# Two squared-relu MLPs: the relu moved to ScalarE without the norm's factor, the factor squared applied as a column of numbers where results are added

## The chip, the cores and the metric

The kernel runs on one core of a Trainium2 chip. The metric is the device time of one execution in microseconds (us). A core has TensorE (PE in the profile; PEld is its weight load), VectorE (DVE), ScalarE (ACT), GpSimd (POOL) and a queue processor for transfers (SP, SyncE). Sums of matmuls are collected in PSUM, eight banks of 512 float32 numbers in each of 128 partitions.

## The reference

The whole program is two transformer blocks. The change touches only the MLPs of the second block, of which there are two. All values are float32, with 512 tokens of width 1024 and a hidden width of 4096:

```
def _rmsnorm(x, g):
    y = xf * lax.rsqrt(jnp.mean(xf * xf, axis=-1, keepdims=True) + EPS)
    return (y * g).astype(x.dtype)

def _sqrelu_mlp(h, w1, w2):
    u = jax.nn.relu(h @ w1)
    return (u * u) @ w2

for i in range(DEPTH_2):                     # 2: retention, then chunk attention
    ...
    h = h + _sqrelu_mlp(_rmsnorm(h, mlp_norm_g[i]), mlp_w1[i], mlp_w2[i])
```

Below, r is the factor rsqrt(mean(x²) + eps). It is one number per token and positive, so relu(r·a) = r·relu(a), and r² can be pulled out of the square and out of the second product, which sums over the hidden width and not over tokens.

## The kernel before

**Precision.** Every float32 product is made of three TensorE products of a high and a low part: high·high, low·high, high·low (L925 to L927, helper `three`). So each weight and each activation is first split: ScalarE copies it to a rounded type (`w_hi`, `hid_hi`, `hn_hi`), and VectorE or GpSimd subtracts that from the original (`w_lo`, `hid_lo`, `hn_lo`).

**An MLP** (`mlp` on each engine; stage A runs from about 1048 to 1379 us, stage B from about 1619 to 1949 us) goes through 4 groups of 1024 hidden columns. In a group there are first four "ups" (m = 0 to 3, `mlp_up`): each makes 256 hidden columns for all tokens in a pair of PSUM banks, Y (banks 0, 1) for even m and X (banks 2, 3) for odd m, with 48 matmuls. The activations are x times the gain, without r. Then come seven second products of 24 matmuls each in the order A11, A12, S3, M, A21, S1, S4 (`PRODUCTS`): a Strassen-like scheme with seven instead of eight products, whose sums of blocks of the squared activations are T3, T2, T4, T1 (VectorE, `t3` to `t1`) and whose sums of weight blocks are made by accumulating transfers that POOL issues (`weight_sums`, L892, L896, L898) and by VectorE (`m_sum`, L3063).

**After an up**, VectorE takes the pair of banks, makes max(·, 0) times r (`relu`, L3022, one instruction of 128x1024 into `sq`), and tells with `mlp_up_taken`; ScalarE squares that into `u_squared` (L2169), which lies in the place of `x`; ScalarE then makes the high part (L2178) and VectorE the low part (L3029). r is there as a row for all tokens (`r_bc`), since tokens lie along the columns here.

**The second product** has tokens along the partitions. Its results are added to `x_tok` (x transposed, in `o_buf`) by VectorE's `take` (L3072). In each group there are nine: Q1, Q7, Q6, Q2, Q4 with two banks at once (128x1024), and Q5, Q5+1, Q3, Q3+1 with one bank (128x512). PE waits for some of them before it opens a bank again: M for Q1, A21 for Q7, S1 for Q6, and S4, whose two token tiles share X with S1, for Q5 and Q5+1 (L1445).

**How r is made.** ScalarE squares x, VectorE adds up the eight tiles in `ssq`, and splits the sum in two rounded halves (L2369, L2371). PE spreads their sum to all partitions with two matmuls with ones (`stat_halves`, L968), one before k = 3 and one before k = 4 of the second up of group 0 (`in_second`); ScalarE makes exp(-0.5·ln(·)) of the 128x512 result (`rsqrt`, L1671, L1674). VectorE waits for r before anything else in the MLP (L3074).

**The transposes** of x to `x_tok` also lie in group 0: PE does f = 0 to 3 in the second up, ahead of k = 4 to 7, and f = 4 to 7 in the third up, ahead of k = 0 to 3 (`to_tokens`, L1467, four 128x128 transposes each, banks 4 to 6), and ScalarE copies each to `x_tok` (`token_copy`, L2160). In ScalarE's order copies 0 to 3 stand ahead of the first square and copies 4 to 7 behind its high part. Up m waits at its start until up m-2 is taken (L1407), since it uses the same banks.

**Orders** on each engine are written out by hand; every wait is on a semaphore. The squared r as a column of numbers is already known elsewhere: the retention head uses `stat_columns` (L973): four matmuls with a 128x128 tile of `ssq` as weights and one column of ones, so that token t of each tile lands in partition t.

## Time and profile before

| | us |
|---|---|
| median of 3 timed runs (1957.20 to 1957.37) | 1957.34 |
| the profiled execution, its own time | 1958.46 |
| the profiled execution, its span | 1956.7 |
| PE busy in the span | 1938.3 (99%) |
| DVE busy | 1205.2 (62%) |
| ACT busy | 880.1 (45%) |
| POOL busy | 603.0 (31%) |

A row of a timeline has the start in us from the span's start, the duration in us, engine, line, operation, output and inputs, shape and count; brackets at its end give the idle time of the engine before it and what ended that. Matmuls overlap: a 128x512 matmul is shown with 0.39 us, but the next one starts 0.227 us after it. So PE's pace is read from the distances between starts, not from durations. The same holds for VectorE and ScalarE, where the next instruction starts about 0.08 to 0.11 us before the end of the one before it.

### The profile page before, as it was taken

The page shows a single profiled execution, that of the slowest core. Times are in us where ns is not written, and L with a number is a line of the kernel's source. Part 1 is how long each engine was busy: PE and PEld are TensorE (multiplying, and loading weights), DVE is VectorE, ACT ScalarE, POOL GpSimd, SP SyncE. Part 2 cuts the span into 40 slices and gives each one's busy share as a digit, 9 for nine tenths or more (in the row PEclk, how much of TensorE's full clock was granted, in tenths as well). Part 3 has the DMA queues.
Part 4 walks back from the last instruction along what each step waited for, and adds up shares of the span by engine and source line. Part 5 has one row for each costly group of instructions (what it writes and reads, how often), then busy time and mean ns, then how long its engine had stood idle before and what let it go on. Part 6 is the DMA issues. An engine that isn't in the chain of part 4 may idle for free.

```text
span 1956.7 us, 23662 instructions
## 1 busy us (share of the span) xinstructions
PE 1938.3 (99%) x9216; PEld 1609.5 (82%) x9216; DVE 1205.2 (62%) x1701; ACT 880.1 (45%) x1284; POOL 603.0 (31%) x442
## 2 busy tenths in 40 slices
PE   8999999999999999999999999999999999999998
PEld 7877878888888888888888888888888888888886
DVE  7667763332257854545455857668566676866757
ACT  7445543332234552525245534444455555444435
POOL 2333645455455335353533000000333341000000
PEclk9999999999999999999999999999999999999999
DMA  5312367276322322222225557465322226746553
GB/s 164 94 44 76 97 98 116 93 123 112 94 86 87 119 76 94 79 87 85 86 86 151 128 173 179 123 172 129 107 86 85 86 65 183 173 128 172 122 179 86
DMA packets 166338, 221.31 MB, mean 113 GB/s; under 512 B 4640, under 2 KB 120096, under 8 KB 166112
## 3 DMA queue, kind: packets, MB, share of 16 engines
q1 hardware_dynamic: 151728, 190.52, 30.0%
q0 software_dynamic: 12928, 25.71, 7.7%
q10 hardware_dynamic: 1584, 3.74, 4.3%
q8 instruction: 66, 1.08, 0.2%
q14 instruction: 32, 0.26, 0.0%
HBM read 214.84 MB, written 4.72 MB: 112 GB/s over the span
## 4 chain that ended last, share of the span: by engine, by line
PE 89%; DVE 4%; ACT 2%; issue 2%; POOL 1%; DMA 1%; SPq 0%; DVEq 0%; ACTq 0%; POOLq 0%
PE ps L925 28%; PE ps L927 28%; PE ps L926 28%; PE ps L1097 1%; PE ps L1127 1%; POOL w_lo L819 1%; PE ps L1136 1%; PE ps L1137 1%; PE ps L1114 1%; DVE scr L2601 1%; DMA aux<-in_mlp_w 0%; PE ps L1467 0%; ACT w_hi L1612 0%; ACT w_hi L1630 0%; DVE w_lo L3011 0%
## 5 line engine op out<-in xcount | busy, mean ns | idle before, releaser
L819 POOL TENSOR_TENSOR w_lo<-raw,w_hi 128x512 fp32r<-128x512 f32 x376 | 529.8, 1440 | 667.4 <-ACT w_hi L1612 667.4
L925 PE MATMUL ps<-hn_hi,w_hi 128*128 128x512 f32 x1524 | 602.4, 395 | 2.2 <-DVE hn_lo L2710 1.7
L927 PE MATMUL ps<-hn_hi,w_lo 128*128 128x512 f32 x1524 | 593.8, 390 | 0.0
L926 PE MATMUL ps<-hn_lo,w_hi 128*128 128x512 f32 x1524 | 593.7, 390 | 0.0
L925 PEld LDWEIGHTS ps<-hn_hi,w_hi 128*128 128x128 f32 x1524 | 286.4, 188 | 66.3 <-issue 4.1
L927 PEld LDWEIGHTS ps<-hn_hi,w_lo 128*128 128x128 f32 x1524 | 286.2, 188 | 60.6
L926 PEld LDWEIGHTS ps<-hn_lo,w_hi 128*128 128x128 f32 x1524 | 286.5, 188 | 58.9 <-issue 1.7
L1612 ACT ACTIVATE w_hi<-raw 128x2048 fp32r<-128x2048 f32 (+1 forms) x98 | 186.0, 1898 | 286.9 <-PE ps L927 286.8
L1630 ACT ACTIVATE w_hi<-raw 128x1024 fp32r<-128x1024 f32 x112 | 116.1, 1056 | 205.2 <-PE ps L927 205.0
L925 PE MATMUL ps<-w_hi,hid_hi 128*128 128x512 f32 x456 | 177.7, 390 | 0.2
L926 PE MATMUL ps<-w_lo,hid_hi 128*128 128x512 f32 x456 | 177.4, 389 | 0.0
L927 PE MATMUL ps<-w_hi,hid_lo 128*128 128x512 f32 x456 | 177.4, 389 | 0.0
L3011 DVE TENSOR_TENSOR w_lo<-raw,w_hi 128x1024 fp32r<-128x1024 f32 x104 | 126.2, 1223 | 67.6 <-ACT w_hi L1630 59.3
L926 PE MATMUL ps<-hid_lo,w_hi 128*128 128x512 f32 x392 | 152.7, 390 | 0.0
L925 PE MATMUL ps<-hid_hi,w_hi 128*128 128x512 f32 x376 | 147.8, 393 | 0.1
L927 PE MATMUL ps<-hid_hi,w_lo 128*128 128x512 f32 x376 | 146.4, 389 | 0.0
L2414 DVE TENSOR_TENSOR scr<-ps,scr 128x512 f32<-128x512 f32 x42 | 27.1, 686 | 138.7 <-PE ps L927 135.3
L896 POOL DMA_DIRECT2D raw<-in_mlp_w x8 | 10.3, 1286 | 305.5 <-DMA raw<-in_mlp_w 305.5
L925 PEld LDWEIGHTS ps<-w_hi,hid_hi 128*128 128x128 f32 x456 | 85.6, 188 | 18.6 <-DVE hid_lo L2537 0.6
L927 PEld LDWEIGHTS ps<-w_hi,hid_lo 128*128 128x128 f32 x456 | 85.6, 188 | 17.8
L926 PEld LDWEIGHTS ps<-w_lo,hid_hi 128*128 128x128 f32 x456 | 85.6, 188 | 17.8
L3029 DVE TENSOR_TENSOR hid_lo<-x,hid_hi 128x512 fp32r<-128x512 f32 (+1 forms) x96 | 74.7, 778 | 32.6 <-ACT hid_hi L2178 31.8
(357 smaller groups left out, 2849.8 us busy)
## 6 DMA issues: line engine op xcount, KB each, us to landing
raw<-in_mlp_w SPq DMA_DIRECT2D x56, 1024.0 KB, 5.4
raw<-in_ret_w_in SPq DMA_DIRECT2D x24, 1024.0 KB, 5.2
aux<-in_mlp_w POOLq DMA_DIRECT2D x16, 1024.0 KB, 8.9
raw<-in_att_w_in SPq DMA_DIRECT2D x12, 1024.0 KB, 5.5
raw<-in_w_gate SPq DMA_DIRECT2D x11, 1024.0 KB, 5.4
raw<-in_w_up SPq DMA_DIRECT2D x11, 1024.0 KB, 5.3
raw<-in_w_down SPq DMA_DIRECT2D x8, 1024.0 KB, 8.0
raw<-in_ret_w_out SPq DMA_DIRECT2D x8, 1024.0 KB, 5.0
```

The lines of the kernel that those rows point to most:

```text
L819: ins = pool.tensor_tensor(w_lo[:, slot, at], raw[:, slot, at], w_hi[:, slot, at].bitcast(F32), ALU.subtract)
L925: pe.matmul(o, hi, rhs_hi, start=start, stop=False, skip_group_check=True)
L926: pe.matmul(o, hi, rhs_lo, start=False, stop=False, skip_group_check=True)
L927: return pe.matmul(o, lo, rhs_hi, start=False, stop=stop, skip_group_check=True)
L1097: ins = pe.matmul(a.score_ps(b, t), q[:, t * P:(t + 1) * P], k[:, 0:(t + 1) * P], start=(n == 0), stop=(n == last), skip_group_check=True)
L1114: ins = pe.matmul(a.score_ps(b, t), q[:, t * P:(t + 1) * P], k[:, 0:(t + 1) * P], start=(nth == 0 and n == 0 and t != 0), stop=(nth == 1 a ...
L1127: ins = pe.transpose(a.trans_ps(b, j)[:, (t - j) * P:(t - j + 1) * P], a.score_sb(b, t)[:, j * P:(j + 1) * P], ident[:, :])
L1612: act.activation(w_hi[:, c.slot, 0:columns], raw[:, c.slot, 0:columns], ACT.Copy)\
L1630: act.activation(w_hi[:, ml.slot(g, b), HALVES[half]], half_source(ml, g, b, half), ACT.Copy)\
L2414: dve.tensor_tensor(dst, ps[:, g.bank(m), :], r, ALU.mult).then_inc(pair_free[g.pair], 1)
L3011: dve.tensor_tensor(w_lo[:, slot, at], half_source(ml, g, b, half), w_hi[:, slot, at].bitcast(F32), ALU.subtract).then_inc(s["w_lo_ready"], 1)
L3029: dve.tensor_tensor(lo_part, src, hi_part.bitcast(F32), ALU.subtract).then_inc(s["mlp_lo"], 1)
```

## The change

The MLP's statistics are now made by `stat_columns` (before k = 3 of the second up, into bank 7), so neither rounded halves nor a spread row are made. ScalarE makes r² from it in three small instructions (ln, exp with scale -1, and a negated copy) into `r_two`: four columns of r², four of -r². The relu of each up is done by ScalarE, from the PSUM banks straight into `u_squared`, and its square in place. VectorE's `relu` and its wait for r go. `take` becomes one `scalar_tensor_tensor` for each bank: bank times the token tile's column of ±r², plus `x_tok`. VectorE waits once per MLP for `r_two`, ahead of the first half of M in group 0.

```diff
-    def __init__(self, prev, n, split, halves=False, by_tokens=False):
+    def __init__(self, prev, n, split, halves=False, by_tokens=False, columns=False):
-        self.index = prev.index + (not by_tokens) if prev else 0
+        self.index = prev.index + (not by_tokens and not columns) if prev else 0
-N_MLPA = Norm(N_RET, 8, 8, halves=True)
+N_MLPA = Norm(N_RET, 8, 8, columns=True)
-N_MLPB = Norm(N_ATT, 8, 8, halves=True)
+N_MLPB = Norm(N_ATT, 8, 8, columns=True)
+        r_two = sb("r_two", [P, 8])
-            def stat_columns(norm):
+            def stat_columns(norm, bank=6):
-                    if 3 <= k < 5:
-                        stat_halves(norm, k - 3)
+                    if k == 3:
+                        stat_columns(norm, 7)
+                def r_for_tokens():
+                    act.wait_ge(s["col_stat"], 2 + ml.layer)
+                    act.activation(r_two[:, 0:4], ps[:, 7, 0:4], ACT.Ln, scale=1.0 / D, bias=eps[:, 0:1])\
+                        .then_inc(s["col_ln"], 1)
+                    act.wait_ge(s["col_ln"], 2 * ml.layer + 2)
+                    act.activation(r_two[:, 0:4], r_two[:, 0:4], ACT.Exp, scale=-1.0).then_inc(s["mlp_r"], 1)
+                    act.wait_ge(s["mlp_r"], 2 * ml.layer + 1)
+                    act.activation(r_two[:, 4:8], r_two[:, 0:4], ACT.Copy, scale=-1.0).then_inc(s["mlp_r"], 1)
                 def squared(g, m):
-                    act.wait_ge(s["mlp_up_taken"], ml.ups(g, m))
+                    bank, u = (Y, X)[m % 2], u_squared[:, 2 * m:2 * m + 2, :]
+                    act.wait_ge(s["group_done"], ml.done(g, m, 1))
                     if g == 0:
                         act.wait_ge(s["x_t"], turned + 2 * m + 2)
-                    act.activation(u_squared[:, 2 * m:2 * m + 2, :], sq, ACT.Square).then_inc(s["mlp_sq"], 1)
+                    act.activation(u, ps[:, bank:bank + 2, :], ACT.Relu).then_inc(s["mlp_up_taken"], 1)
+                    act.wait_ge(s["mlp_up_taken"], ml.ups(g, m))
+                    act.activation(u, u, ACT.Square).then_inc(s["mlp_sq"], 1)
                         if g == 0 and m == 0:
-                            rsqrt(norm, D)
+                            r_for_tokens()
                             for f in range(4):
                                 token_copy(f)
                         squared(g, m)
-                def relu(g, m):
-                    ...
-                    dve.scalar_tensor_tensor(sq, ps[:, bank:bank + 2, :], 0.0, r_bc.unsqueeze(1).to_broadcast([P, 2, S]),
-                                             ALU.max, ALU.mult).then_inc(s["mlp_up_taken"], 1)
                 def take(g, product, b, half, f, t, bank, op, tiles=slice(0, 2)):
                     ...
-                    o = token_block(f, t)[:, tiles, :]
-                    dve.tensor_tensor(o, o, ps[:, bank + tiles.start:bank + tiles.stop, :], op).then_inc(s["mlp_taken"], 1)
-                dve.wait_ge(s["norm_r"], norm.index + 1)
+                    for n in range(tiles.start, tiles.stop):
+                        o, at = token_block(f, t)[:, n, :], 2 * t + n + (0 if op is ALU.add else 4)
+                        ins = dve.scalar_tensor_tensor(o, ps[:, bank + n, :], r_two[:, at:at + 1], o, ALU.mult, ALU.add)
+                    ins.then_inc(s["mlp_taken"], 1)
                         half_lo(ml, g, m + 2, 0)
-                        relu(g, m)
                         half_lo(ml, g, m + 2, 1)
                     if g == 0:
                         dve.wait_ge(s["x_copied"], kept + KD)
+                        dve.wait_ge(s["mlp_r"], 2 * ml.layer + 2)
```

The numbers that `col_ln` waits for elsewhere are renumbered; nothing else moves.

## Rows read from the trace of the kernel before

**Rows 1.** The page, part 1: busy time of PE, share, instructions.
```profile
PE 1938.3 (99%) x9216; PEld 1609.5 (82%) x9216; DVE 1205.2 (62%) x1701; ACT 880.1 (45%) x1284; POOL 603.0 (31%) x442
```

**Rows 2.** Windows, all but the ends of MLP A: start:end, length, busy us (instructions), granted clock, DMA share.
```profile
1061.00:1378.00 317.00, 317.00 (x1424) 262.76 (x1423) 217.81 (x230) 144.90 (x171) 14.12 (x11) 1.00 0.57 150
```

**Rows 3.** Timeline, PE: the first statistics matmul in the second up, and the next.
```profile
1061.45 0.39 PE L968 MATMUL ps<-sq_halves,ones_r 128*128 128x512 f32 x1
1061.68 0.39 PE L925 MATMUL ps<-hn_hi,w_hi 128*128 128x512 f32 x1
```

**Rows 4.** Timeline, PE: the column statistics of the retention head.
```profile
662.17 1.03 PE L977 MATMUL ps<-ones_r,scr 128*128 128x1 f32 x8
663.06 0.48 PE L968 MATMUL ps<-sq_halves,ones_r 128*128 128x512 f32 x1
663.38 0.39 PE L925 MATMUL ps<-hn_hi,w_hi 128*128 128x512 f32 x1
```

**Rows 5.** Timeline, PE and PEld: transposes 3 and 4, and the third up's start.
```profile
1068.75 0.60 PE L1467 MATMUL ps<-ident,x 128*128 128x128 f32 x4
...
1070.58 0.60 PE L1467 MATMUL ps<-ident,x 128*128 128x128 f32 x4
...
1070.35 0.59 PEld L1467 LDWEIGHTS ps<-ident,x 128*128 128x128 f32 x4
```

**Rows 6.** Timeline, ACT, in the same stretch; then DVE's first relu.
```profile
1069.39 0.60 ACT L2160 ACTIVATE o_buf<-ps 128x512 f32<-128x512 f32 x1 [1.23 <-PE ps L1467]
1069.88 1.05 ACT L2169 ACTIVATE x<-scr 128x1024 f32<-128x1024 f32 x1
...
1066.44 1.22 DVE L3022 SCALAR_TENSOR_TENSOR scr<-ps,scr 128x1024 f32<-128x1024 f32 x1
```

**Rows 7.** Timeline, DVE, attention's start: instructions with a column of numbers, from PSUM.
```profile
1378.13 1.41 DVE L3143 SCALAR_TENSOR_TENSOR hn_lo<-ps,gains,hn_hi 128x512 fp32r<-128x512 f32 x2 [1.29 <-ACT hn_hi L2227]
1379.46 0.68 DVE L3072 TENSOR_TENSOR o_buf<-o_buf,ps 128x512 f32<-128x512 f32 x1
```

**Rows 8.** Timeline, DVE, MLP A, group 1: the takes, and the weight halves of S4.
```profile
1188.45 1.22 DVE L3072 TENSOR_TENSOR o_buf<-o_buf,ps 128x1024 f32<-128x1024 f32 x1
1189.58 1.22 DVE L3063 TENSOR_TENSOR aux<-aux,hid_rest 128x1024 f32<-128x1024 f32 x1
...
1201.69 1.22 DVE L3072 TENSOR_TENSOR o_buf<-o_buf,ps 128x1024 f32<-128x1024 f32 x1
1203.28 2.36 DVE L3011 TENSOR_TENSOR w_lo<-aux,w_hi 128x1024 fp32r<-128x1024 f32 x2 [0.37 <-ACT w_hi L1630]
1205.55 2.01 DVE L3072 TENSOR_TENSOR o_buf<-o_buf,ps 128x1024 f32<-128x1024 f32 x2
```

**Rows 9.** Timeline, POOL, ACT and PEld, same group: transfer for S4, S4's first weights.
```profile
1193.46 1.28 POOL L898 DMA_DIRECT2D aux<-in_mlp_w  x1 [19.48 <-DVE w_lo L3011]
...
1202.18 2.17 ACT L1630 ACTIVATE w_hi<-aux 128x1024 fp32r<-128x1024 f32 x2 [3.27 <-DMA aux<-in_mlp_w]
...
1208.24 0.19 PEld L925 LDWEIGHTS ps<-w_hi,hid_hi 128*128 128x128 f32 x1
```

**Rows 10.** Timeline, DVE and PEld, MLP B, group 1: the same place.
```profile
1777.64 2.01 DVE L3072 TENSOR_TENSOR o_buf<-o_buf,ps 128x1024 f32<-128x1024 f32 x2
...
1779.94 0.19 PEld L925 LDWEIGHTS ps<-w_hi,hid_hi 128*128 128x128 f32 x1
```

**Rows 11.** Timeline, PE, PEld, DVE, MLP B, group 0: the same place.
```profile
1697.96 0.39 PE L927 MATMUL ps<-w_hi,hid_lo 128*128 128x512 f32 x1
1698.44 0.50 PE L925 MATMUL ps<-w_hi,hid_hi 128*128 128x512 f32 x1
...
1696.38 2.80 DVE L3072 TENSOR_TENSOR o_buf<-o_buf,ps 128x1024 f32<-128x1024 f32 x3
...
1698.43 0.19 PEld L925 LDWEIGHTS ps<-w_hi,hid_hi 128*128 128x128 f32 x1 [0.51 <-DVE o_buf L3072]
```

**Rows 12.** Timeline, ACT and DVE, the last 12 us.
```profile
1944.60 0.29 ACT L2329 ACTIVATE small<-small 128x1 f32<-128x1 f32 x1 [0.36 <-DVE small L3317]
```

More of the change, by code:

```diff
@@ L298 @@
  gain_pair old_hi old_lo apart_done apart_scaled apart_sum gate_old_done gate_e_hi gate_e_lo gate_sig gate_read
- mlp_up_taken mlp_sq mlp_sum mlp_hi mlp_lo mlp_taken s3_in s3_added a21_in s1_added m_summed s4_added
+ mlp_up_taken mlp_r mlp_sq mlp_sum mlp_hi mlp_lo mlp_taken s3_in s3_added a21_in s1_added m_summed s4_added
  att_in_hi att_in_lo tab_scaled ffn_silu ffn_part token_sq token_sum r_diagonal r_spread r_row fin_weighed fin_left fin_right fin_whole""".split()
@@ L971, in stat_halves @@
                     ins.then_inc(s["norm_stat"], 1)
-            def stat_columns(norm):
+            def stat_columns(norm, bank=6):
                 pe.wait_ge(s["norm_acc"], norm.acc0 + norm.n - 1)
                 for t in range(4):
-                    ins = pe.matmul(ps[:, 6, t:t + 1], ssq[:, t * P:(t + 1) * P], ones[:, 0:1], start=True, stop=True)
+                    ins = pe.matmul(ps[:, bank, t:t + 1], ssq[:, t * P:(t + 1) * P], ones[:, 0:1], start=True, stop=True)
                 ins.then_inc(s["col_stat"], 1)
@@ L1656, in rsqrt_columns @@
                     .then_inc(s["col_ln"], 1)
-                act.wait_ge(s["col_ln"], nth + 1)
+                act.wait_ge(s["col_ln"], 2 * nth + 1)
                 act.activation(r_col[:, 0:4], r_col[:, 0:4], ACT.Exp, scale=-0.5).then_inc(s["col_r"], 1)
@@ L2330, in token_rsqrt @@
                     .then_inc(s["col_ln"], 1)
-                act.wait_ge(s["col_ln"], 3 + t)
+                act.wait_ge(s["col_ln"], 5 + t)
                 act.activation(r_col[:, t:t + 1], r_col[:, t:t + 1], ACT.Exp, scale=-0.5).then_inc(s["col_r"], 1)
@@ L3014, in mlp @@
             def mlp(ml, norm, kept, finish):
-                def relu(g, m):
-                    bank = (Y, X)[m % 2]
-                    dve.wait_ge(s["group_done"], ml.done(g, m, 1))
-                    if ml.ups(g, m) > 1:
-                        dve.wait_ge(s["mlp_sq"], ml.ups(g, m) - 1)
-                    dve.scalar_tensor_tensor(sq, ps[:, bank:bank + 2, :], 0.0, r_bc.unsqueeze(1).to_broadcast([P, 2, S]),
-                                             ALU.max, ALU.mult).then_inc(s["mlp_up_taken"], 1)
                 def part_lo(g, what, n):
```

## The prediction, made before the changed kernel was run

> **What bounds the kernel now.** I read the busy times first. TensorE is busy for 99% of the span [rows 1], so the end is set by its own work, and no other engine's load counts unless it makes PE wait. Then the windows: over nearly the whole of MLP A, PE is busy for all of 317.00 us, at a granted clock of 1.00 (the upper of the two levels, 2.4 GHz), while VectorE is at 218 us and ScalarE at 145 us [rows 2]. Then PE's timeline. Its 128x512 matmuls start 0.227 us apart [rows 3], and in both MLPs I found only one place where this pace is lost to a wait: in MLP B, group 0, at S4, where the next matmul starts 0.476 us after the last one instead of 0.227, and its weight load waited 0.51 us for a `take` [rows 11]. So there is at most 0.4 us of stall that the change could take away, and the question is what it adds to PE's stream and which new waits reach PE.
>
> **The PE's own work.** Removed per MLP: two 128x512 matmuls with ones, 2 x 0.227 = 0.45 us [rows 3]. Added: four column matmuls of the kind that the retention head has. They are eight instructions there, from 662.17 to 663.06, 0.89 us, and the matmul after them is followed at 0.32 us instead of 0.227 [rows 4], another 0.09. Net +0.53 us per MLP, +1.06 us for two. All of it is on the path, since PE is. The bounds: 0.89 us may hold a short wait for the sum of squares, so +0.3 to +0.6 each. The sum is there early enough in both MLPs, so nothing is waited for.
> What the row shows is 0.11 us for each one-column matmul. The Trainium skill (TensorE: Matmul & The Clock Gate, section Back-to-back issue gap) gives about 60 cycles for 1 to 64 columns, which is 25 ns at 2.4 GHz; with that the four would cost an estimated 0.2 us and the change would save about 0.15 us of PE per MLP. The same page (section LDWEIGHTS) has about columns/1.2 ns for a weight load, 107 ns for 128, and that is what the trace agrees with: every column matmul brings its own 128x128 weights.
>
> **The third up waits for ScalarE.** This is the new wait. Up 2 of group 0 may start only when up 0 has been taken. Before, VectorE did that at 1066.44 to 1067.66 [rows 6], three us early. Now it is the relu of ScalarE, and in ScalarE's order it stands behind `token_copy` 0 to 3, the last of which waits for the fourth set of transposes. In the trace: those transposes start at 1068.75, the third up's first instruction (transposes 4) at 1070.58, its weight load at 1070.35 [rows 5]. ScalarE starts copy 3 at 1069.39, that is 0.64 after the transposes, and can start the next instruction at 1069.88 [rows 6]. That next one is now the relu. No row shows a relu of 128x1024 from PSUM; the square of that size takes 1.05 from SBUF, the copy of 128x512 from PSUM 0.60 [rows 6]. I take 1.03, with 1.0 and 1.22 (VectorE's [rows 6]) as the ends. It ends at 1070.91. A weight load follows its release by 0.05 us (1698.38, the end of the second of the three takes there, to 1698.43 [rows 11]), so it starts at 1070.96 instead of 1070.35. Of such a delay 0.1 to 0.2 is swallowed, because the weight load runs ahead of its matmul: in [rows 11] a weight load 0.47 late cost PE 0.25 at the first matmul and 0.11 at the second. So 0.61 late costs about 0.5 us. All times shift together when the column matmuls come ahead, so the distance stays. +0.5 us per MLP, **+1.0 us** for two; bounds 0.3 and 0.7 each. Up 3's wait for up 1 has about 3 us to spare, as has A12's wait for up 3: 0 us. Queued behind the relu on ScalarE are the square, the high part and copies 4 to 7; transposes 7 wait for copy 4 (done at about 1073.7, needed at 1076.4): 0 us.
>
> **ScalarE in the other ups.** From group 1 on VectorE took a finished up at once, and ScalarE meanwhile made the high half of a weight block. Now the relu is behind that half: square and parts come about 0.9 us later. The parts of up 3 are needed only at A12's second half, 3.5 us after they are ready, and in the products ScalarE then waits for PE again (S3's second half), which takes up the delay. 0 us. The ceiling, were that cover gone, is 0.9 us for each group.
> A rule that speaks against the change: the Trainium skill (ScalarE: Activation LUTs, section Rules for kernel authors) says to put relu on VectorE. It argues with bfloat16 modes; here the rows show float32 work of the same size at 1.22 us on VectorE and 1.05 us on ScalarE [rows 6], so the rule costs nothing in this kernel; the order on ScalarE does.
>
> **VectorE's takes.** VectorE loses 4 relus of 1.22 us per group, but they lie among the ups, where nothing waits for it. The cost is in the products. Two instructions with a column of numbers from PSUM occupy 1.33 us (1378.13 to 1379.46 [rows 7]) and the second ends 1.41 after the first starts; the 128x1024 `take` occupies 1.13 to 1.14 and takes 1.22 [rows 8]. So +0.2 us for each of the five two-bank takes and 0.06 for a one-bank take (0.745 against 0.69). From Q1 to Q2 VectorE has next to no idle time, so four takes (Q1, Q7, Q6, Q2) move its arrival at S4's weight halves by 0.78 us; the 0.37 to 0.46 us of idle time there [rows 8] swallow part of it. The transfer that makes S4's weights starts behind VectorE's low half of M [rows 9], which only Q1 delays: +0.2. Then Q4 and Q5 lie between these halves and PE's S4: +0.25 more at Q5's end.
> Group 1 of MLP A: Q2 starts at 1201.69; 1.135 + 0.78 later, at 1203.61, VectorE comes to S4 instead of at 1203.28: +0.33, and Q5 ends 0.58 later. It ended at 1207.56; S4's weight load started at 1208.24 [rows 8, 9] and needs 0.05, so the slack was 0.63: 0 us. Worked out so for the eight groups (first and most critical: [rows 8 to 10]) the slack is 0.62 to 0.66 in five, with shifts of 0.58 to 0.65; 0.38 in group 0 of MLP A, with a shift of 0.49, where the 0.115 that is swallowed just covers it; 0.24 in group 1 of MLP B (Q5 ends at 1779.65, load at 1779.94 [rows 10]), where the transfer leads and the shift is 0.45: 0.45 - 0.24 - 0.115 = 0.1 us; and none in group 0 of MLP B, which stalls already: +0.45 us. **Sum +0.55 us**, bounds 0 (a landing that is early again) and 3 (all groups 0.4 late).
>
> **The tail.** In the last group Q4 ends 0.55 later (0.35 at S4's halves and 0.2 in itself); ScalarE's squares for the final norm follow it, and had 0.36 us to spare before VectorE's mean [rows 12]: +0.2 at the end. The last two takes are one-bank takes in VectorE's chain: +0.12. Together +0.3 us, bounds 0.1 and 0.6.
>
> **At nothing:** VectorE's cast and subtraction for the halves, and its wait for r, go from where PE never waited. Three small instructions for r² (0.7 us) replace two of 128x512 on ScalarE, in time that it spends waiting for transposes. VectorE's wait for r² comes 40 us after it is made.
>
> **Sum:** 1.06 + 1.0 + 0.55 + 0.3 = 2.9 us. The profiled execution would go from 1958.46 (span 1956.7) to 1961.4 (span 1959.6). Its time is 1.1 us above the median of the timed runs; I add to the median: 1957.34 + 2.9 = 1960.2, or +0.15%. A measurement of this kernel tells about 0.2% (3.9 us) from no change, so this is "the same".
>
> **The rivals.**
> *A slower kernel (above 1961.3).* The takes reach PE in every group. This decides from the point where Q5 ends 0.75 us later (slack 0.64 plus the 0.115 swallowed), and my shifts are only 0.1 to 0.2 below that in five groups. If a two-instruction take occupied 1.5 instead of 1.33 us, S4's halves would come at +1.5 - 0.4, Q5 at +1.45, and each group would pay about 0.5 to 0.7 us: 8 x 0.5 = 4 us and with the other terms 1957.3 + 2.4 + 4 = 1963.7. For it: margins this small. Against it: POOL, which shares VectorE's work in other stages, is busy for 14 of 317 us here [rows 2].
> *Cheaper than said (1957.5 to 1959.3).* The new wait costs 0.3 and the column sums 0.3 per MLP, and S4 is not reached: 0.6 + 0.6 + 0 + 0.2 = 1.6, 1958.9. It needs a quicker relu and an earlier landing of the one late transfer.
> *Faster (below 1953.4).* It would have to take 4 us off PE's own stream. The freed 39 us of VectorE (32 x 1.22) can give back only the 0.4 us stall [rows 2, 11]: 1957.0 even if nothing were added.
> *It does not do what it says:* r² could be late and hold VectorE at its wait; it is made by about 1064 and needed at about 1105.
>
> **How the numbers follow.** Forecast (1959.3 to 1961.2) 0.63, cheaper 0.15, slower 0.19, faster 0.03. The range leaves out no more than 2 in 10: 1958.3 (all lower bounds: 0.6 + 0.6 + 0 + 0.1 gives 1.3, and a little is left out) to 1963.2. Same: 0.63 + 0.15 = 0.78.
>
> **What would show it.** Right: after the change L977 has 24 instructions in all and L968 two fewer per MLP; PE waits twice for ScalarE's relu, ahead of transposes 4, some 0.5 us each; takes in pairs of 0.745 us at 0.665 apart; S4 waits in MLP B for `take` in groups 0 and 1. VectorE's busy time falls by about 28 us and ScalarE's rises by about 31. Wrong: a PE wait at A12 or for part lows (ScalarE's order), waits at S4 in all eight groups (slower rival), or a relu far from 1.03 us.

## The result, and the profile after

| | before | after |
|---|---|---|
| median, 20 runs each | 1957.45 | 1960.31 |
| lowest to highest | 1956.83 to 1958.90 | 1959.02 to 1962.73 |
| profiled execution, own time | 1958.46 | 1959.21 |
| its span | 1956.7 | 1957.4 |

The ratio is 1.0015, with a 95% interval of 1.0008 to 1.0022: 2.9 us more, where the sum had said 2.9. Two things in the table are not explained by that sum. The spans of the two profiled executions differ by 0.7 us only, and the times of the changed kernel lie almost twice as far apart as those of the one before. All medians and ratios here and below leave out two executions that took far longer than all others, one of "relu early" (3955 us) and one of the kernel before beside it (6937 us).

The page of the changed kernel, part 1; it answers to [rows 1]:
```profile
PE 1938.8 (99%) x9228; PEld 1610.0 (82%) x9228; DVE 1174.0 (60%) x1705; ACT 909.2 (46%) x1318; POOL 604.3 (31%) x442
```
PE has 12 instructions more: in each MLP eight column instructions for two of 128x512. VectorE lost 31.2 us, ScalarE gained 29.1.

The timeline of the changed kernel, PE, at the statistics of MLP A (start, duration, engine, line, operation, tiles, shape, count). It answers to [rows 3, 4]:
```profile
1060.93 0.39 PE L928 MATMUL ps<-hn_hi,w_lo 128*128 128x512 f32 x1
1061.16 0.94 PE L978 MATMUL ps<-ones_r,scr 128*128 128x1 f32 x8
1061.97 0.49 PE L926 MATMUL ps<-hn_hi,w_hi 128*128 128x512 f32 x1
1062.29 0.40 PE L927 MATMUL ps<-hn_lo,w_hi 128*128 128x512 f32 x1
```
The eight take 0.81 us from their first start to the next matmul, and that one is followed 0.32 instead of 0.227 later. I laid all matmuls of this trace beside those of before, one by one, and followed the difference of their starts. Over the statistics it grows by 0.46 us in MLP A and 0.47 in MLP B.

The same stretch some 9 us later, ACT, PE and PEld (in brackets the idle time before, and what ended it). It answers to [rows 5, 6]:
```profile
1069.57 0.60 ACT L2161 ACTIVATE o_buf<-ps 128x512 f32<-128x512 f32 x1 [1.24 <-PE ps L1468]
1070.07 1.02 ACT L2181 ACTIVATE x<-ps 128x1024 f32<-128x1024 f32 x1
...
1070.53 0.40 PE L928 MATMUL ps<-hn_hi,w_lo 128*128 128x512 f32 x1
1071.14 0.66 PE L1468 MATMUL ps<-ident,x 128*128 128x128 f32 x4 [0.21 <-ACT x L2181]
...
1071.14 0.42 PEld L1468 LDWEIGHTS ps<-ident,x 128*128 128x128 f32 x4 [0.64 <-ACT x L2181]
```
This is the new wait. The third up's first instruction starts 0.61 after the matmul ahead of it. The difference of the starts grows by 0.43 us here, and by 0.43 in MLP B: 0.37 of it at the first of the four transposes, 0.06 at the second.

The timeline of the changed kernel in MLP B, group 2, from the transfer that makes S4's weights to PE's S4. It answers to [rows 8, 9, 11]:
```profile
1846.90 1.28 POOL L899 DMA_DIRECT2D aux<-in_mlp_w  x1 [19.26 <-DVE w_lo L3025]
...
1856.44 2.01 ACT L1631 ACTIVATE w_hi<-aux 128x1024 fp32r<-128x1024 f32 x2 [4.27 <-DMA aux<-in_mlp_w]
...
1855.51 1.40 DVE L3078 SCALAR_TENSOR_TENSOR o_buf<-ps,r_two,o_buf 128x512 f32<-128x512 f32 x2
1857.53 2.36 DVE L3025 TENSOR_TENSOR w_lo<-aux,w_hi 128x1024 fp32r<-128x1024 f32 x2 [0.62 <-ACT w_hi L1631]
1859.81 3.12 DVE L3078 SCALAR_TENSOR_TENSOR o_buf<-ps,r_two,o_buf 128x512 f32<-128x512 f32 x4
...
1862.12 0.50 PE L926 MATMUL ps<-w_hi,hid_hi 128*128 128x512 f32 x1 [0.23 <-DVE o_buf L3078]
1862.46 0.40 PE L927 MATMUL ps<-w_lo,hid_hi 128*128 128x512 f32 x1
```
The transfer is issued at 1846.90, and ScalarE starts on its result 9.54 us later; VectorE's halves, then Q4 and Q5, follow without a gap, and PE waits. It loses 0.56 us here and 0.17 in group 1. Group 0, the one place with a loss before (0.38 us, [rows 11]), loses nothing.

Waits of the weight load from 1060 us to the end, changed kernel (what is waited for, us in total, times, longest), the rows that are new:
```profile
PEld ps L1468 <- ACT x L2181: 1.3, 2, 0.6
PEld ps L926 <- DVE o_buf L3078: 1.0, 2, 0.7
```
So the terms of the profiled execution are 0.93 (columns) + 0.86 (relu) + 0.35 (S4: 0.73 less 0.38) + 0.19 (from the start of the last matmul to the end: 8.28 against 8.09) = 2.3 us. Its span grew by 0.7, because three waits of some 0.4 us in the attention, which the kernel before had in its profile, aren't in this one (1.3 us), and the start was 0.3 us shorter. The start varies by more than that between executions; how far the attention's waits are chance is taken up in the last section.

### The profile page after: what moved, and what is told of

Same layout as the page of the kernel before. It is cut to its first block, busy times and chain, and to the rows that moved or that the text cites. A ratio compares the mean times of both kernels' runs of the same rounds, so it can differ in the third digit from the quotient of the medians.

```text
span 1957.4 us, 23691 instructions
## 1 busy us (share of the span) xinstructions
PE 1938.8 (99%) x9228; PEld 1610.0 (82%) x9228; DVE 1174.0 (60%) x1705; ACT 909.2 (46%) x1318; POOL 604.3 (31%) x442
## 4 chain that ended last, share of the span: by engine, by line
PE 90%; DVE 4%; ACT 3%; issue 2%; POOL 1%; DMA 1%; SPq 0%; DVEq 0%; POOLq 0%; ACTq 0%
PE ps L926 28%; PE ps L928 28%; PE ps L927 28%; PE ps L1098 1%; PE ps L1128 1%; POOL w_lo L820 1%; PE ps L1137 1%; PE ps L1138 1%; PE ps L1115 1%; DMA aux<-in_mlp_w 0%; ACT scr L1842 0%; ACT w_hi L1613 0%; PE ps L1468 0%; DMA raw<-in_w_in 0%; DVE hn_lo L2877 0%
```

## The experiments

Each kernel ran 11 times (the columns twice 9 times). "Before" is the median of the kernel before on the same chip; the spans are those of the profiled executions. A difference of the spans alone is not much to go by: the first 12 us alone were up to 2.3 us longer in some executions than in others.

| kernel | median | before | ratio, 95% | span |
|---|---|---|---|---|
| the change again | 1960.81 | 1958.26 | 1.0013 [1.0004, 1.0022] | 1958.8 |
| relu early | 1960.65 | 1958.53 | 1.0011 [1.0001, 1.0020] | 1956.8 |
| takes alone | 1959.50 | 1958.53 | 1.0005 [0.9996, 1.0015] | 1957.7 |
| plain takes | 1959.74 | 1958.53 | 1.0006 [0.9997, 1.0015] | 1957.9 |
| columns twice | 1963.42 | 1958.53 | 1.0024 [1.0014, 1.0034] | 1961.1 |
| relu early, Q4 later | 1958.95 | 1958.26 | 1.0003 [0.9994, 1.0012] | 1957.6 |
| before, Q4 later | 1958.30 | 1958.26 | 1.0000 [0.9991, 1.0009] | 1956.1 |
| statistics over tokens, Q4 later | 1957.77 | 1958.26 | 0.9998 [0.9989, 1.0007] | 1955.2 |
| the same again | 1957.52 | 1958.02 | 0.9997 [0.9988, 1.0006] | 1955.4 |
| statistics over tokens, Q4 first | 1959.63 | 1958.02 | 1.0008 [0.9999, 1.0017] | 1959.0 |

**The relu early.** The theory is that the new wait is one of order on ScalarE: the first relu stands behind the copies. The relu now goes between copies 1 and 2, and nothing else moves:
```diff
                             for f in range(4):
+                                if f == 2:
+                                    taken_relu(g, m)
                                 token_copy(f)
```


> The changed kernel with one order changed: ScalarE does the relu of up 0 of group 0 between token copies 1 and 2 instead of after copy 3. Theory A (the loss is a sum of three separate PE-side terms: column sums 0.5 us per MLP, the wait of the third up for the relu 0.4 us per MLP, the takes at S4 and in the tail 0.6 to 0.9 in all): both PE waits ahead of transposes 4 (weight load idle 0.6 us each in the changed kernel) are gone, PE is 0.4 us earlier from there in each MLP, and the median falls by 0.75 us, from 1960.3 to 1959.5. Theory B (nearly all of the 2.9 us comes from the takes, and a wait that is removed ahead of them is only paid later, at S4): the waits are gone, the median stays at 1960.3 within 0.2. Theory C (the loss is ScalarE's later squares): no change either, 1960.3.

ACT and PE of this kernel at the same place:
```profile
1066.63 1.02 ACT L2181 ACTIVATE x<-ps 128x1024 f32<-128x1024 f32 x1
1067.96 0.60 ACT L2161 ACTIVATE o_buf<-ps 128x512 f32<-128x512 f32 x1 [0.31 <-PE ps L1468]
1069.79 0.60 ACT L2161 ACTIVATE o_buf<-ps 128x512 f32<-128x512 f32 x1 [1.23 <-PE ps L1468]
...
1070.75 0.39 PE L928 MATMUL ps<-hn_hi,w_lo 128*128 128x512 f32 x1
1070.98 0.60 PE L1468 MATMUL ps<-ident,x 128*128 128x128 f32 x4
```
The relu lies in a hole of ScalarE, 3.4 us earlier, the copies behind it still have to wait for PE, and transposes 4 start 0.23 after the matmul ahead of them. The wait is gone in both MLPs. So its cause is shown: the place in ScalarE's order, not the length of the relu. Nor is it paid back later: over the whole of MLP A the difference of the starts grows by 0.48 us here and by 0.89 in the change. The medians (+2.1 us here, +2.9 and +2.6 for the change) lean the same way but can't tell 0.86 us; the trace does.

**The takes alone.** The kernel before, with its takes made as in the change, and columns of +1 and -1 in place of r²:
```diff
-                    o = token_block(f, t)[:, tiles, :]
-                    dve.tensor_tensor(o, o, ps[:, bank + tiles.start:bank + tiles.stop, :], op).then_inc(s["mlp_taken"], 1)
+                    for n in range(tiles.start, tiles.stop):
+                        o, at = token_block(f, t)[:, n, :], 2 * t + n + (0 if op is ALU.add else 4)
+                        ins = dve.scalar_tensor_tensor(o, ps[:, bank + n, :], r_two[:, at:at + 1], o, ALU.mult, ALU.add)
+                    ins.then_inc(s["mlp_taken"], 1)
```


> The kernel before, with one part of the change: each take is done by one instruction per bank with a column of numbers, which holds 1 or -1, so the result is the same. Relu by VectorE with r, statistics by halves. Theory A: PE's stream is that of before up to S4; at S4 PE waits in the groups where the transfer leads (0.1 to 0.5 us each in one to three of eight groups), the tail is 0.2 to 0.3 longer: median 1957.45 + 0.9 = 1958.3. Theory B (the takes are nearly all of it): 1960. If takes cost PE nothing: 1957.5.

**The plain takes.** The opposite: the changed kernel with the takes of before. It leaves out the factor r², so what it adds to x is not the MLP's result; only its time is of use.
```diff
-                    for n in range(tiles.start, tiles.stop):
-                        o, at = token_block(f, t)[:, n, :], 2 * t + n + (0 if op is ALU.add else 4)
-                        ins = dve.scalar_tensor_tensor(o, ps[:, bank + n, :], r_two[:, at:at + 1], o, ALU.mult, ALU.add)
-                    ins.then_inc(s["mlp_taken"], 1)
+                    o = token_block(f, t)[:, tiles, :]
+                    dve.tensor_tensor(o, o, ps[:, bank + tiles.start:bank + tiles.stop, :], op).then_inc(s["mlp_taken"], 1)
```


> The changed kernel with the takes of before (one instruction for both banks, no factor), so r squared is left out of what is added to x; all else, the making of r squared too, is as in the changed kernel. Theory A: the column sums and the two waits for the relu stay, S4 waits only where it did before, the tail is that of before: 1960.3 - 0.9 = 1959.4, and the spread of the runs (1959.0 to 1962.7) shrinks towards that of before (1956.8 to 1958.9), since it is S4 that passes on when a transfer lands. Theory B: 1957.5. Theory C: 1960.3.

The takes by shape (duration in ns: shortest, median, longest; first and last start), the takes alone and then, in the kernel with the plain ones:
```profile
L3074 DVE SCALAR_TENSOR_TENSOR o_buf<-ps,r_two,o_buf x112: 673/748/755, 1107.6 to 1951.4; 128x512 f32<-128x512 f32 x112
```
```profile
L3077 DVE TENSOR_TENSOR o_buf<-o_buf,ps x72: 620/1214/1222, 1107.8 to 1951.7; 128x1024 f32<-128x1024 f32 x40, 128x512 f32<-128x512 f32 x32
```
The medians say +1.0 for the takes alone and +1.2 for all the rest of the change, each with an interval of some 2 us to either side; together that is 2.2, where the whole change has 2.6 and 2.9. What a take costs PE can't be read from them. It can from a table over the seven traces with this order of takes. The first number is the time from POOL's issue of S4's transfer to ScalarE's first high half, the second the loss of PE at S4 in that group. In MLP A the transfer always took 8.2 to 8.9 us and PE lost at most 0.03 in these kernels; these are the four groups of MLP B:
```
                              group 0       group 1       group 2       group 3
old takes   before            9.64  0.38    9.12  0       8.68  0       8.64  0
            plain takes       8.70  0       9.35  0       9.82  0.37    8.44  0
new takes   change            8.64  0       9.19  0.17    9.53  0.56    8.46  0
            change again      8.42  0       9.33  0.31   10.00  0.99    8.50  0
            relu early        8.78  0       8.83  0       9.70  0.72    8.34  0
            takes alone       8.60  0.02    9.51  0.51    8.44  0       8.61  0
            columns twice     8.30  0       8.77  0       9.30  0.31    9.66  0.69
```
With the new takes every transfer over 9.0 us costs about what it is over: 9.19 costs 0.17, 9.33 costs 0.31, 9.51 costs 0.51 and 10.00 costs 0.99. With the old takes one of 9.35 costs nothing and one of 9.82 costs 0.37; in group 0, the tightest, 9.64 costs 0.38. So what the new takes do is to lower what PE tolerates, outside group 0, from some 9.4 to 9.0 us, by about the 0.45 us that the prediction had as the shift where the transfer leads. Whether this also spreads the times is not shown: the plain takes were expected to lie closer together than the change, and their 11 runs lie over 2.6 us, those of the change again over 2.4, and those of the kernel before in the same session as the plain takes over 3.9.

Which group gets a late transfer has a pattern that the traces show. The DMA view of such a transfer in the kernel before (9.64 us) has, besides the transfer's own queue, this line (packets, MB, share):
```profile
q8 instruction: 1, 0.02, 0.6%
```
It is one packet of 16 KB that brings instructions. In the twelve traces there are 96 transfers for S4. In 23 of them such a packet falls between 4.9 and 8.0 us after the issue, and 22 of these are the ones that took 9.1 to 10.0 us, one took 8.8. All the other 73 took 8.2 to 8.8. None of the 48 in MLP A has a packet at that place, and none of them was late. Where the packets fall goes with the program: the change had both its late transfers in groups 1 and 2 in both of its profiles, and the first two kernels with statistics over tokens below, which are one kernel, both theirs in groups 0 and 1. No run moved a packet by itself, so that it makes the transfer late is argued from this agreement; and how late it is (9.53 and 10.00 for the same group of the same kernel) still varies between executions.

**The change again.** The same kernel, profiled a second time.

> The changed kernel once more, on the chip and beside the runs of the kernels of this call, for a second profile. Two things are asked. First, S4: theory A says that the group that makes PE wait there is chosen by when the transfer of its weights lands, so in another profile another group waits (landing after about 9.1 us), with the takes themselves unchanged. Second, attention: in the first profile PE waits less there for VectorE (L2615, one of the four multiplications behind GpSimd's start) than in the profile of before, 1.3 us in three places. If the change caused that, the second profile shows the same; if it is a race between the two engines that falls either way, it may show one to three of these waits again. Median as before: 1960.3, or the other kernels' shift on this chip added.

The timeline, VectorE, MLP B, group 2:
```profile
1858.97 2.36 DVE L3025 TENSOR_TENSOR w_lo<-aux,w_hi 128x1024 fp32r<-128x1024 f32 x2 [1.09 <-ACT w_hi L1631]
1861.25 3.12 DVE L3078 SCALAR_TENSOR_TENSOR o_buf<-ps,r_two,o_buf 128x512 f32<-128x512 f32 x4
```
VectorE sits idle for 1.09 us until the transfer is there (0.62 in the first profile), and PE loses 0.99. Columns 0.47 and 0.47, relu 0.43 and 0.43: these two repeat to 0.01 us. S4 doesn't: 1.30 in all against 0.73. But the expectation that another group would wait was wrong: they are groups 1 and 2 again. The span of this execution is 2.1 us above that of the first profile of before.

**The columns twice.** The four column matmuls once more, into columns of bank 7 that nobody reads:
```diff
                     if k == 3:
+                        for t in range(4):
+                            pe.wait_ge(s["norm_acc"], norm.acc0 + norm.n - 1)
+                            pe.matmul(ps[:, 7, 4 + t:5 + t], ssq[:, t * P:(t + 1) * P], ones[:, 0:1], start=True, stop=True)
                         stat_columns(norm, 7)
```


> The changed kernel with the four column matmuls done twice in each MLP (the first time into other columns of the same bank, which nobody reads). This measures their price by itself. Theory A: 0.11 us for each of eight instructions, because each loads its own 128x128 weights: PE falls back by 0.89 us more in each MLP, median 1960.3 + 1.8 = 1962.1. If a one-column matmul costs only its few columns (about 0.03 us each, 0.2 for the eight): 1960.3 + 0.4 = 1960.7.

PE of this kernel, at the statistics:
```profile
1062.06 0.39 PE L928 MATMUL ps<-hn_hi,w_lo 128*128 128x512 f32 x1
1062.29 0.95 PE L1480 MATMUL ps<-ones_r,scr 128*128 128x1 f32 x8
1063.10 1.03 PE L978 MATMUL ps<-ones_r,scr 128*128 128x1 f32 x8
1063.99 0.49 PE L926 MATMUL ps<-hn_hi,w_hi 128*128 128x512 f32 x1
```
Sixteen instructions in 1.70 us, 0.106 each. Beside the change the difference of the starts is 0.89 us larger in MLP A and 0.89 in MLP B. Against its own before the median stands at +4.9 us, the change's at +2.9 and +2.6: 2.0 to 2.3 more, of which the columns are 1.8. So four columns cost 0.89 us of PE, all of it on the path, and the step of the prediction that priced them from the retention head is shown right by a measurement of its own.

**Q4 later.** If PE loses at S4 because Q4 stands between the weight halves and Q5, then with Q5 and Q5+1 first, in groups 0 to 2, the loss goes, since PE's S4 needs these and not Q4. Made on the kernel with the early relu, and, as a control, on the kernel before (the counts that others wait for are renumbered in `taken`):
```diff
-                    take(g, ml.Q4, ml.A21, 1, 1, 0, Y, ALU.add)
+                    if last:
+                        take(g, ml.Q4, ml.A21, 1, 1, 0, Y, ALU.add)
...
                     take(g, ml.Q5 + 1, ml.S1, 1, 1, 1, X, ALU.subtract, slice(1, 2))
                     if not last:
+                        take(g, ml.Q4, ml.A21, 1, 1, 0, Y, ALU.add)
```


> The kernel of e1 (relu of up 0 between token copies 1 and 2), and in groups 0 to 2 of each MLP the two-bank take Q4 stands after Q5 and Q5+1 instead of ahead of them, so PE's S4 no longer waits for Q4. Theory A (the rest of the loss at S4 is the chain landing, weight halves, Q4, Q5): Q5 ends 1.4 to 1.5 us earlier in these groups, PE waits at S4 in none of the first three groups of an MLP even where the transfer lands after 9.5 us, and the median is 0.5 us below that of e1: 1.0 to 1.5 us above the kernel before. Rival (a take that is moved back makes PE wait at the next group's first up): waits there instead, no gain over e1.

> The kernel before with only that order changed: Q4 after Q5 and Q5+1 in groups 0 to 2. Theory A: its one wait at S4 (0.4 us in MLP B) goes, nothing else changes: 0.3 to 0.4 us faster than before, hardly more than noise in the median, but to be seen in the profile as no wait at S4 with a landing of up to 9.6 us. Rival: the wait returns at the next up.

VectorE, MLP B, group 2, in the kernel with the early relu and this order:
```profile
1858.73 2.36 DVE L3035 TENSOR_TENSOR w_lo<-aux,w_hi 128x1024 fp32r<-128x1024 f32 x2 [1.01 <-ACT w_hi L1633]
1861.01 0.75 DVE L3088 SCALAR_TENSOR_TENSOR o_buf<-ps,r_two,o_buf 128x512 f32<-128x512 f32 x1
1862.74 2.27 DVE L3088 SCALAR_TENSOR_TENSOR o_buf<-ps,r_two,o_buf 128x512 f32<-128x512 f32 x3 [0.99 <-PE ps L930]
```
The transfer is again very late here (9.92 us), VectorE idles for it for 1.01 us, as in the second profile of the change, and yet PE loses nothing: after Q5, VectorE now waits 0.99 us for PE. No group of either kernel loses time at S4, with transfers of up to 9.92 and 9.55 us (the last group of an MLP, whose order is as it was, had none over 8.5). For the kernel before it is worth 0.38 us in its trace, and its median doesn't move; it had next to nothing to win there. For the kernel with the early relu it is worth what S4 costs: over both MLPs the difference of the starts to the kernel before grows by 0.56 us, where it grew by 1.29. The medians, +2.1 and +0.7 us over before in two sessions, lean the same way. No wait came up at the next group's first up.

**The statistics over tokens.** What is left are the columns. The norm ahead of the attention already sums the squares over tokens; done so here, from `x_tok`, ScalarE squares each half of a token tile with a running sum once it is copied (eight of 128x512 in each MLP), and the column matmuls go, along with the squares and sums ahead of the MLP:
```diff
-N_MLPA = Norm(N_RET, 8, 8, columns=True)
+N_MLPA = Norm(N_RET, 0, 8, by_tokens=True)
-                    if k == 3:
-                        stat_columns(norm, 7)
+                def token_mean(t, half):
+                    act.wait_ge(s["x_copied"], turned + 4 * half + 4)
+                    if half:
+                        act.wait_ge(s["gains_ready"], 2 + 8 * ml.layer + t + 1)
+                    act.activation(scr[:, t, :], x_tok[:, t, 512 * half:512 * half + 512], ACT.Square,
+                                   accum_out=mx[:, 2 * t + half:2 * t + half + 1]).then_inc(s["gains_ready"], 1)
```
It ran three times: twice with Q4 later, once with Q4 first.

> The kernel of e5, and the sums of squares are made without TensorE: ScalarE squares x_tok (tokens along the partitions) with a running sum per token, half a row ahead of each of token copies 4 to 7 and the other half after the high part of up 1, VectorE adds the two halves, ScalarE makes r squared ahead of the T parts of group 0. No column matmuls, no squares and sums of x ahead of the MLP. Theory A (PE's own stream is the price of everything): PE is 0.95 us ahead of e5 per MLP, that is 0.45 per MLP ahead of the kernel before: 1957.5 - 0.9 - 0.4 (no S4 wait) + 0.2 (tail) = 1956.4, 1.1 us below the kernel before. Rival (ScalarE is too full in group 0): PE waits for the relu of up 1 or of up 3 in group 0, 1 us or more in each MLP, and the time is that of the kernel before or above.

> The kernel of e8 once more (statistics by ScalarE over tokens, Q4 after Q5+1, relu early), beside runs of the kernel before on this chip, since its gain over the kernel before (0.5 us, 0.02%) was within the interval. Theory A: PE again falls behind nowhere in the MLPs, S4 never waits, and the profile's last matmul comes 1.2 us or more ahead of that of before apart from what start and attention do; median 0.5 to 1.2 us below the kernel before. If the first result was noise: the median equals that of before.

> The kernel of e8 with Q4 back ahead of Q5 in all groups, as in the changed kernel. Theory A: where a transfer for S4 lands after 9.1 us (one or two groups of MLP B) PE waits at S4 again, 0.2 to 1.0 us in all, so the median is 0.4 to 1.0 us above that of e8 and the runs are wider apart; nothing else differs. Rival (S4's waits don't reach the end): same median as e8.

ScalarE in the third up of MLP A, with Q4 later, a part (the second row of each square reads its sum):
```profile
1071.28 0.61 ACT L2176 ACTIVATE scr<-o_buf 128x512 f32<-128x512 f32 x1
1071.80 0.19 ACT L2176 ACTIVATION_READ_ACCUMULATOR scr<-o_buf 128x1 f32 x1
1071.89 0.57 ACT L2157 ACTIVATE o_buf<-ps 128x512 f32<-128x512 f32 x1
```
The squares in the third up fill holes of ScalarE; the four behind up 1 don't, as is shown below. PE now does no statistics: over this place it gains 0.46 us on the kernel before in each MLP, whose two matmuls with ones are gone too (0.45 was expected). Over both MLPs it gains 1.25 us in both profiles (S4's 0.38 is in that), and its last matmul comes 1.63 and 1.42 us earlier than in before. The medians are 0.5 us below before twice, which the intervals don't tell from no difference. Against the change on the same chip the first of the two is 3.0 us lower (1957.77 and 1960.81).

With Q4 first the same kernel is 2.1 us slower on the same chip. PE's wait there in MLP B, group 0, and ScalarE's and VectorE's rows ahead of it:
```profile
1694.41 2.01 ACT L1629 ACTIVATE w_hi<-aux 128x1024 fp32r<-128x1024 f32 x2 [5.46 <-DMA aux<-in_mlp_w]
...
1695.50 2.36 DVE L3040 TENSOR_TENSOR w_lo<-aux,w_hi 128x1024 fp32r<-128x1024 f32 x2 [0.95 <-ACT w_hi L1629]
1697.78 3.11 DVE L3093 SCALAR_TENSOR_TENSOR o_buf<-ps,r_two,o_buf 128x512 f32<-128x512 f32 x4
...
1700.09 0.50 PE L926 MATMUL ps<-w_hi,hid_hi 128*128 128x512 f32 x1 [1.42 <-DVE o_buf L3093]
```
The transfer took 9.87 us and PE lost 1.73; another 0.72 was lost in group 0 of MLP A, where the transfer took a usual 8.59, and 0.40 in group 1 of MLP B (9.40 us), which is what the table has for such a transfer. The median was expected to be 0.4 to 1.0 us above the kernel with Q4 later, and is 2.1 above it; the two groups 0 are what was not foreseen. The rows point to ScalarE's order again. Behind up 1 it now does four squares with their sums, 2.45 us, ahead of the weight halves and the relu of up 2. This kernel in MLP A:
```profile
1085.11 0.62 ACT L2174 ACTIVATE scr<-o_buf 128x512 f32<-128x512 f32 x1
1085.63 0.19 ACT L2174 ACTIVATION_READ_ACCUMULATOR scr<-o_buf 128x1 f32 x1
1085.72 1.99 ACT L1629 ACTIVATE w_hi<-raw 128x1024 fp32r<-128x1024 f32 x2
1087.62 1.01 ACT L2183 ACTIVATE x<-ps 128x1024 f32<-128x1024 f32 x1
```
And the kernel with the early relu:
```profile
1084.01 1.06 ACT L1631 ACTIVATE w_hi<-raw 128x1024 fp32r<-128x1024 f32 x1 [0.37 <-PE ps L928]
1084.98 1.00 ACT L2181 ACTIVATE x<-ps 128x1024 f32<-128x1024 f32 x1
```
The relu of up 2 comes 2.64 us later, where PE at this place is only 0.67 later than in that kernel. The parts of the T sums and VectorE's low halves follow the relus, and POOL's transfer for S4 is issued 1.44 us later in MLP A, so 0.77 later than PE. That is about what each group 0 lost beyond the table (0.72, and 1.73 against some 0.9). So what takes this kernel over the margin seems to be its squares and not its takes; no run moved the squares by themselves.

## Why the prediction was right, and where it wasn't

**The column sums: right.** Predicted 0.53 per MLP, measured 0.46 and 0.47, and 0.89 for four further ones, where the retention head's row gave 0.89. The eight take 0.81 here and 0.89 there: the retention row did hold a short wait, as the prediction had allowed. The rule of the Trainium skill (TensorE: Matmul & The Clock Gate, section Back-to-back issue gap) of about 60 cycles for so few columns would have made this part a gain of 0.15 us; the trace gives 0.106 us per instruction, which is 4 times as much. The same page's weight load of 107 ns (section LDWEIGHTS) is what these matmuls cost. That it is the load and not a fixed price of a matmul is argued from this agreement; no run has narrow matmuls that share their weights.

**The wait for ScalarE's relu: right, 0.07 too high in size.** The relu of 128x1024 from PSUM has a row now, 32 of them in the changed kernel:
```profile
L2181 ACT ACTIVATE x<-ps x32: 1005/1011/1021, 1070.1 to 1912.5; 128x1024 f32<-128x1024 f32 x32
```
I had taken 1.03; it is 1.01. The weight load came at 1071.14. Without the wait it would have come 0.23 us before its matmul, which would have started 0.23 after the one at 1070.53, so at 1070.53: it was 0.61 us late, as said. PE lost 0.43. The load's head start swallowed 0.18 us, where I had named 0.1 to 0.2 and taken 0.11 off; that makes 0.14 us over the two MLPs. No wait at A12 and none for other parts came up, so ScalarE's order in the other ups did cost nothing.

**The takes: right in size, wrong in place.** The row of the changed kernel:
```profile
L3078 DVE SCALAR_TENSOR_TENSOR o_buf<-ps,r_two,o_buf x112: 671/743/751, 1107.5 to 1951.1; 128x512 f32<-128x512 f32 x112
```
0.743 for 0.745, and the pairs take 1.40 for 1.41. The shift of Q5 in group 1 of MLP A came as 0.52 us for 0.58. The step that failed is the one behind it. I worked out a slack for each of the eight groups from the landings of one profile of the kernel before, as if the change left them where they were, and put 0.45 us on group 0 of MLP B and 0.1 on group 1. In the changed kernel's profile groups 1 and 2 lost instead, and in its second profile the same two lost 1.30, which net of before's loss is 0.92 against 0.35. The late transfers had moved with the packets of instructions, and how late they are varies by up to half a microsecond. The right way to put this term is the tolerance before (9.4) and after (9.0), and the number of transfers over 9.0 us (one or two of 8 in each of the twelve profiles, all in MLP B). That gives about 0.4 us more for each transfer that was over the tolerance already, and up to that for those between. That 0.55 was near the mean of the two profiles (0.64) is luck: group 0 of MLP B, which held most of it, lost nothing, and two others did. The bounds of 0 to 3 stood for that.

**The tail: 0.2 for 0.3.** I did not split it further.

**The sum: 2.3 in the profiled execution and 2.9 in the second one, for 2.9.** The columns are 0.1 lower than said, the wait 0.14 and the tail 0.1, in both; S4 is 0.2 lower in the first and 0.4 higher in the second, which makes up for the others. So the mechanism is right, and that the sum is right to 0.1 us is luck in part. The medians differ by 2.9 and 2.6, and they also hold what the attention's waits did on average, which no run tells. That the first profile's span grew by only 0.7 is where a reader might have gone wrong the other way.

**The engines' busy time.** VectorE's fell by 31.2 (said 28), ScalarE's rose by 29.1 (said 31). Neither mattered: the 30 us that left VectorE bought no PE time. Windows over nearly all of MLP A, the changed kernel, in the columns of [rows 2]:
```profile
1061.00:1378.00 317.00, 316.79 (x1426) 262.47 (x1425) 202.40 (x233) 158.85 (x186) 14.12 (x11) 1.00 0.57 149
```
VectorE has 202 us of work in these 317 and had 218; PE is at its pace as before, less the one wait.

**The rivals.** The slower kernel, with a loss in every group, didn't come: transfers of usual length (8.2 to 8.9 us) cost at most 0.03 us in any kernel with the column matmuls. The margin was as small as I thought: the takes alone cost 0.03 us in group 0 of MLP A, where the prediction had the shift just covered. The kernel with the statistics over tokens and Q4 first shows what it looks like once the margin is crossed. Cheaper and faster didn't come.

## What to carry to other kernels

Work that moves to an idle engine takes its place in that engine's order, and its price is where in the order it stands: the same relu cost 0.43 us behind the copies and nothing between them. Where a chain hangs on a transfer, read its landing from several executions, look what else the DMA engines carried, and ask how late it may be, not whether it was late; and among the steps behind it put first the one that the bounding engine waits for. A matmul of one column isn't cheap if it brings weights of its own: here each instruction cost 0.11 us.

## What the runs showed of the hardware that I had not expected

**Two engines in a race in the attention.** The three waits that left the profile are at three like places of the attention. VectorE and POOL at the first, the kernel before:
```profile
1449.64 2.37 DVE L2601 TENSOR_SCALAR scr<-scr,small 128x128 f32<-128x128 f32 x4
...
1450.44 5.21 POOL L819 TENSOR_TENSOR w_lo<-raw,w_hi 128x512 fp32r<-128x512 f32 x4 [9.31 <-ACT w_hi L1612]
```
And the changed kernel:
```profile
1450.22 1.28 DVE L2615 TENSOR_SCALAR scr<-scr,small 128x128 f32<-128x128 f32 x4
...
1451.02 5.84 POOL L820 TENSOR_TENSOR w_lo<-raw,w_hi 128x512 fp32r<-128x512 f32 x4 [9.33 <-ACT w_hi L1613]
```
Same instructions, and POOL starts 0.80 us after VectorE in both. In the one VectorE's four take 2.37 us, and PE waits for them; in the other they take 1.28, and POOL's take 0.63 longer. Of the three places, these had PE's wait: before 3, the change 0 and in its second profile 1, takes alone 3, plain takes 2, columns twice 1, relu early 0, relu early with Q4 later 0, before with Q4 later 1, statistics over tokens 2, 1 and 0. Both outcomes come with the relu on VectorE and on ScalarE, and in different executions of one kernel, so the change doesn't decide it alone; what does is open. Whether the change makes the wait rarer is open too: it came at 7 of 9 places with the relu on VectorE and at 7 of 27 with the relu on ScalarE. That the two engines get in each other's way fits what the Trainium skill (SBUF — State Buffer, section SBUF: two separate sides) says of a pair of ports that they share: it is locked for a whole instruction by the one that starts first. The page says this of certain kinds of instructions; that these are of them is not shown here. It is worth up to 1.3 us of a span, as much as half of the change.

**The landing of one transfer.** 1 MB, added to what is there, issued by POOL: 8.2 to 8.9 us in MLP A in all twelve traces, 8.3 to 10.0 us in MLP B, with the same instructions. All 22 that took over 9.0 us had a 16 KB packet of instructions landing among theirs, 5 to 8 us after the issue; the same kernel profiled twice had it in the same groups.
